# Expert products strip by strip, and the weights of expert 2 and of the last expert in whole loads

## What is computed

```python
# per expert e, for the tokens x routed to it
h = silu(x @ w_gate[e]) * (x @ w_up[e])     # w_gate, w_up: 1024 x 512
y = h @ w_down[e]                            # w_down: 512 x 1024
out = sum over the 2 experts of a token: gate weight * y
```

## Time and profile before

| | us |
|---|---|
| median of three timed runs | 4315.75 |
| lowest and highest of them | 4313.86, 4319.55 |
| the profiled execution, its own time | 4336.46 |
| its span in the trace | 4334.6 |
| PE busy (90% of the span) | 3896.4 |

### The profile page before, as it was taken

The page is one execution under the profiler, slowest core; times in us unless marked ns, Lnnn a source line. Parts: engine busy times, 40 slices in busy tenths (PEclk is TensorE's granted clock), DMA queues, the critical chain, the costliest instruction groups (busy, mean ns, idle before and its releaser), DMA issues. The chain is left out here.

```text
span 4334.6 us, 78138 instructions
## 1 busy us (share of the span) xinstructions
PE 3896.4 (90%) x33934; PEld 2475.1 (57%) x33934; DVE 2106.2 (49%) x3087; ACT 1006.4 (23%) x1749; POOL 620.7 (14%) x456
## 2 busy tenths in 40 slices
PE   7999998899999998999996999876999999699973
PEld 4555654445556545566544777543666665487742
DVE  3555356455555554555565222115666787422214
ACT  2333223133331221222210000003444541000002
POOL 2322011032211100000000211101221300111111
PEclk9999999999999999999997999987999999799986
DMA  4233202332231234544523999983000121699996
GB/s 131 95 108 99 62 20 88 86 112 93 98 98 30 88 108 133 88 78 79 105 85 123 377 417 380 419 356 101 16 1 16 40 70 75 236 417 391 403 424 269
DMA packets 260177, 694.97 MB, mean 160 GB/s; under 512 B 59467, under 2 KB 185043, under 8 KB 234103
## 3 DMA queue, kind: packets, MB, share of 16 engines
q1 hardware_dynamic: 245447, 645.79, 42.1%
q0 software_dynamic: 13056, 39.86, 2.5%
q10 hardware_dynamic: 1328, 4.24, 0.3%
HBM read 617.21 MB, written 64.08 MB: 157 GB/s over the span
## 5 line engine op out<-in xcount | busy, mean ns | idle before, releaser
L512 PE MATMUL ps<-sb_xT,sb_work 128*128 128x512 f32 x768 | 358.8, 605 | 8.6 <-ACT sb_x_tok L854 5.5
L512 PE MATMUL ps<-sb_mixT,sb_work 128*128 128x512 f32 x768 | 357.2, 602 | 8.6 <-ACT sb_x_tok L854 5.5
L2739 DVE TENSOR_TENSOR sb_work<-sb_work,ps 128x256 f32<-128x256 f32 (+2 forms) x66 | 33.6, 510 | 678.0 <-ACT sb_work L2726 678.0
L2726 ACT ACTIVATE sb_work<-ps 128x256 f32<-128x256 f32 (+2 forms) x66 | 30.0, 455 | 1032.6 <-PE ps L2694 1032.6
L1664 PE MATMUL ps<-sb_xT,sb_work 128*128 128x512 f32 x512 | 236.2, 600 | 0.0
L2694 PE MATMUL ps<-sb_work,sb_xT 128*32 128x256 f32 x3136 | 194.9, 398 | 37.0 <-DMA sb_work<-moe_w_up 23.3
L2694 PE MATMUL ps<-sb_work,sb_mixT 128*32 128x256 f32 x3136 | 196.1, 399 | 35.6 <-DMA sb_work<-moe_w_up 22.3
L512 PEld LDWEIGHTS ps<-sb_xT,sb_work 128*128 128x128 f32 x768 | 138.4, 192 | 148.3 <-issue 131.5
L512 PEld LDWEIGHTS ps<-sb_mixT,sb_work 128*128 128x128 f32 x768 | 138.0, 191 | 148.2 <-issue 131.4
L2709 PE MATMUL ps<-sb_work 128*32 128x256 f32 x3776 | 222.0, 379 | 0.0
L2151 DVE TENSOR_REDUCE sb_cols<-ps 128x1 f32<-128x1024 f32 x128 | 150.7, 1219 | 85.7 <-PE ps L1994 85.6
(11 more groups left out here) (497 smaller groups left out, 7019.1 us busy)
## 6 DMA issues: line engine op xcount, KB each, us to landing
sb_work<-moe_w_down SPq DMA_DIRECT2D x42, 2048.0 KB
sb_work<-moe_w_gate SPq DMA_DIRECT2D x30, 2048.0 KB
sb_work<-moe_w_up SPq DMA_DIRECT2D x30, 2048.0 KB
sb_xT<-moe_w_gate SPq DMA_DIRECT2D x15, 2048.0 KB
sb_xT<-moe_w_up SPq DMA_DIRECT2D x15, 2048.0 KB
sb_mixT<-moe_w_gate SPq DMA_DIRECT2D x15, 2048.0 KB
sb_mixT<-moe_w_up SPq DMA_DIRECT2D x15, 2048.0 KB
sb_work<-w_in SPq DMA_DIRECT2D x56, 512.0 KB, 4.3
```

The costliest lines, as they stand in the source:

```text
L512: last = pe.matmul(m.ps[:, bank, :], b.w[i][:, k, :], m.xT[:, k, half * HALF:(half + 1) * HALF], start=(k == 0), stop=(k == NK - 1))
L2726: act.activation(b.act[n % 2][:, 0:strips[n], :], strip_sums(2 + 2 * (n % 2))[:, 0:strips[n], 0:P], ACT.Silu).then_inc(silued, 1)
L2739: dve.tensor_tensor(act, act, strip_sums(2 + 2 * (n % 2))[:, 0:strips[n], P:2 * P], ALU.mult).then_inc(multiplied, 1)
```

## The change

`HALVED` and everything that belongs to it is gone. Gate and up of experts 2 and 31 are loaded like all others, in two transfers of 2 MB. Those of expert 2 wait for `up_ready` of product(0), where the first halves waited for `half_used`. `product` goes strip by strip: for each strip all 8 k tiles, for each k tile the four column tiles, with a start flag on each strip's first k. It waits once for its weights.

```diff
@@ expert_engines, product(n)
-            for half in range(2):
-                if loaded(n, 0, half):
-                    pe.wait_ge(*loaded(n, 0, half))
-                for k in range(half * NK // 2, (half + 1) * NK // 2):
-                    for g in range(strips[n]):
-                        for j in range(QUARTERS):
-                            last = pe.matmul(strip_sums(2 + 2 * (n % 2), tile[j])[:, g, :], b.x_turned[n % 2][:, g, k, :],
-                                             b.gate_up[weights[n] % 2][:, :, k, j * P:(j + 1) * P],
-                                             start=(k == 0 and g % 2 == 0),
-                                             stop=(k == NK - 1 and (g % 2 == 1 or g == strips[n] - 1)))
-                last.then_inc((half_used, up_ready)[half], 1)
+            if loaded(n, 0):
+                pe.wait_ge(*loaded(n, 0))
+            for g in range(strips[n]):
+                for k in range(NK):
+                    for j in range(QUARTERS):
+                        last = pe.matmul(strip_sums(2 + 2 * (n % 2), tile[j])[:, g, :], b.x_turned[n % 2][:, g, k, :],
+                                         b.gate_up[weights[n] % 2][:, :, k, j * P:(j + 1) * P], start=(k == 0), stop=(k == NK - 1))
+            last.then_inc(up_ready, 1)
@@ experts_stage, SP
             def load_gate_up(w):
-                sources = [by_rows(source(w, name)) for name in ("gate", "up")]
-                if w not in HALVED:
-                    for part in range(2):
-                        sp.dma_start(b.gate_up[w % 2][:, part, :, :], sources[part]).then_inc(gate_up_loaded[w % 2], 16)
-                    return
-                for half, landed in enumerate((gate_up_loaded[w % 2], second_loaded)):
-                    k = slice(half * NK // 2, (half + 1) * NK // 2)
-                    if w == HALVED[0]:
-                        sp.wait_ge((half_used, up_ready)[half], 1)
-                    for part in range(2):
-                        sp.dma_start(b.gate_up[w % 2][:, part, k, :], sources[part][:, k, :]).then_inc(landed, 16)
+                for part, name in enumerate(("gate", "up")):
+                    sp.dma_start(b.gate_up[w % 2][:, part, :, :], by_rows(source(w, name))).then_inc(gate_up_loaded[w % 2], 16)
...
             def gate_up_used(n):
                 if last_use(n) and WEIGHTS[n] + 2 < N_EXPERTS:
-                    if n:
-                        sp.wait_ge(up_ready, n + 1)
+                    sp.wait_ge(up_ready, n + 1)
                     load_gate_up(WEIGHTS[n] + 2)
```

More of the change, by code:

```diff
@@ L2257 @@
 LOADS, TURNS, WEIGHTS = weights_in_turn()
-HALVED = (2, N_EXPERTS - 1)
 def last_use(n):
@@ L2669, in expert_engines @@
     x_turned, up_ready, silued, multiplied, y_ready, y_copied = (s[f"signal_{n}"] for n in (0, 2, 3, 4, 5, 6))
-    h_turned, half_used = s["signal_11"], s["signal_13"]
+    h_turned = s["signal_11"]
     stored = s["stored"], s["prefetched"]
@@ L2703, in down @@
                 pe.wait_ge(y_copied, n - 1)
-            if loaded(n, 1, 0):
-                pe.wait_ge(*loaded(n, 1, 0))
+            if loaded(n, 1):
+                pe.wait_ge(*loaded(n, 1))
             for g in range(strips[n]):
@@ L2779, in experts_stage @@
     y_blocks = m.y_dram.rearrange("(p b) d -> p b d", p=P)
-    x_turned, up_ready, y_ready, y_copied, tokens_ready, second_loaded, half_used = (
-        s[f"signal_{n}"] for n in (0, 2, 5, 6, 7, 12, 13))
+    x_turned, up_ready, y_ready, y_copied, tokens_ready = (s[f"signal_{n}"] for n in (0, 2, 5, 6, 7))
     gathered = (m.pool_dma[l]["gathered_a"], m.pool_dma[l]["gathered_b"])
@@ L2848, in _, with loaded @@
                         m.slots[:, g, at:at + 1], 0)).then_inc(gathered[n % 2], 16)
-        def loaded(n, part, half):
+        def loaded(n, part):
             w = WEIGHTS[n]
[L2853 to L2859, removed]
+            if part == 0:
+                return (gate_up_loaded[w % 2], 32 * (w // 2)) if w >= 2 else None
+            return (down_loaded[w % 3], 16 * (w // 3 + (w % 3 == 2))) if w >= 2 else None
         expert_engines(nc, m, block, b, [strips_of(at) for at in TURNS], WEIGHTS, loaded,
@@ L2885, in _ @@
                         pool.sem_inc(tokens_ready, 1)
-                    expert_engines(nc, m, block, b, [4], [0], lambda n, part, half: ((gate_up_loaded, down_loaded)[part][0], (32, 16)[part]),
+                    expert_engines(nc, m, block, b, [4], [0], lambda n, part: ((gate_up_loaded, down_loaded)[part][0], (32, 16)[part]),
                                    lambda n: (tokens_ready, 1))
```

## The result

| | us |
|---|---|
| changed kernel, median of 20 runs (lowest, highest) | 4321.4 (4317.75, 4324.49) |
| kernel before, median of 20 runs beside it | 4315.76 (4312.59, 4319.55) |
| ratio, 95% interval | 1.0013 [1.0007, 1.0019] |
| the changed kernel's profiled execution, its span | 4320.81, 4318.9 |

The change costs 5.6 us. The whole interval lies above 1, so the kernel is slower, but by less than the 0.2% that the prediction took as no change; 11.4 us had been forecast. The profiled execution of the changed kernel is level with its median, while that of the kernel before was 20.7 us above its own. That turns out to matter.

What follows compares the result with a forecast made beforehand. Each expert stage was taken to start with PE and DMA balanced and end bound by loads, at expert 31's landing. 5.71 + 5.71 + 0 + 0 = 11.4 us on 4315.75 gave 4327.2 us, range 4319 to 4332.

Steps and rivals of the forecast that it cites:

- the clock holds: Rival, last product of each stage: PE keeps 2.4 GHz through the wait, 3.45 us per stage, 4322.7 us; chance 0.16.
- signs of being wrong: Whole kernel: last product at 7.11 us, product 2 waiting, three-strip products changing by over 0.1 us, or last landing moving.
- the late load: Rival, start of each stage: expert 2's load lands late and product 2 waits, 4331 to 4337 us; chance 0.10.
- slower by over 0.2%: Whole kernel: chance 0.70 of a time over 4324.4 us.
- The bound and the mechanism: End of each stage: expert 31's landing decides; the first half product must wait for it, costing 5.71 us per stage.
- The size of a product behind the wait: Last product of each stage: 9.37 us at a lowered clock, replacing 3.66 us after the landing.
- Expert 2: Start of each stage: loads leave 5.7 and 7.5 us later, hidden by slack of 1.4 and 1.5 us; cost 0.
- a hole to fill at 2402 us: DMA queues between experts 2 and 3: they run dry, 45 GB/s, and the later expert 2 load uses that bandwidth.
- Strip by strip: Loop order in every product: the array keeps its pace in either order; cost 0.
- "issue" stalls: Idle time in product, 7.9 us in the first stage; rival: strip order removes it, 4311.4 us; chance 0.07.
- The base of the sum: Whole kernel: the added 11.4 us, worked out on the 4336.46 us profile, applies equally to the timed median, 4315.75 us.
- The landing: End of each stage: expert 31's last load lands at the same distance from the stage's start; shift 0.

Runs made afterwards that it cites:

- c3: Kernel before with only expert 31 in whole loads (k outermost, expert 2 in halves), on a chip of the faster kind: 4325.22 us against 4315.89, ratio 1.0022.
- b1: Kernel before with only expert 31 in whole loads (k outermost, expert 2 in halves), on the slower chip: 4346.42 us against 4337.04, ratio 1.0024.
- a2: Changed kernel with product's loops put back to k outermost, experts 2 and 31 still in whole loads: 4320.82 us against 4315.62 before, ratio 1.0011.
- c1: Changed kernel again, no edit, beside three others on one chip: 4322.12 us against 4315.89 for the kernel before, ratio 1.0015.
- c2: Changed kernel plus 64 unused matmul instructions ahead of the wait for expert 31: 4318.71 us against 4315.89 for the kernel before, ratio 1.0006.
- a4: Changed kernel with expert 31 back in halves, its product k outermost with two waits: 4315.99 us against 4315.62 for the kernel before, ratio 1.0001.
- a1: Kernel before, unedited, run again for a second trace: 4315.16 us against 4315.62, ratio 1.0001; traced execution 4311.70 us.
- a3: Kernel before with strips outside k within each half product, experts 2 and 31 still in halves: 4314.55 us against 4315.62, ratio 1.0002.
- b3: Changed kernel plus 64 unused matmul instructions ahead of the wait for expert 31, on the slower chip: 4341.53 us against 4337.04 before, ratio 1.001.
- group b: Four edited kernels run together on one chip, where the kernel before took 4337.04 us; ratios from 0.9998 to 1.0027.

## Why the prediction was right and wrong

**The number** is right by half. 4321.4 us lies in the range of 4319 to 4332, but half of the forecast cost came, and the result lies within the 0.2% to which 0.26 was given. It is nearest to the rival "the clock holds" (4322.7 us), whose condition was not met: both last products of the traced execution took 8.80 us. The terms of the sum that the runs bear out make some 9.3 us; that only 5.6 were paid comes from something for which the prediction has no term. That the number still fell in the range owes as much to luck. Of the signs of being wrong that it had set, two came true: product 2 waited, and the three-strip products became shorter. Its chances do not add up either: the forecast (0.64) and the late load (0.10) both lie above 4324.4 us, so "slower by over 0.2%" had at least 0.74, not 0.70.

**The bound and the mechanism** were right. Both stages end at the landing of expert 31's gate and up, the half product that had run under the transfer moved behind it, and the clock fell in it. c3 and b1 isolate this step where expert 2 stays in halves: +9.3 and +9.4 us, against 11.4 forecast.

**The size of a product behind the wait** was taken too high. The step said 9.37 us, because all eight products with waits of 3.7 us or more had been slow. The ten last products in the profiles of the kernels with a whole last load and nothing ahead of it (the changed kernel, a2, b1, c1, c3) took 7.11 twice, 8.73, 8.80 four times, 8.96, 9.13 and 9.31: mean 8.56 us. With it the step is 8.56 - 3.66 = 4.9 us per stage and 9.8 in all, against 9.3 and 9.4 measured. The rule "3.7 us of wait or more, slow product" was a fit to eight cases and broke once in these ten: 7.11 us behind 3.88 (c3). Three of the ten waits were shorter, 2.01 to 3.40 us, and the six slow products behind the longer ones had a mean of 8.96 us, not 9.37. The rival "the clock holds" was right as an alternative within a stage and wrong as a case for both; c2 shows that its 1.7 us per stage are real.

**Expert 2.** The 0 held as a sum: a4 has this part and the order, and stays within its interval of the kernel before. The working behind it did not hold. In the five traces with the whole load on the faster kind of chip, product 2 waited 0.46 to 0.96 us in nine of ten stages (in a2's second it started 0.3 us late), since the slack of 1.4 us had been read from a trace with slower products. The delay was also not what I counted. On a chip of this kind SP is the later of the two in the first stage. In a1 the first half of product 0 (96 instructions) is done near 2381 us, and SP is still issuing small transfers:

```profile
2380.07 5.63 SPq L2823 DMA_DIRECT2D sb_cols<-scratch_mods  x2
2387.42 0.40 SPq L2806 DMA_DIRECT2D sb_work<-moe_w_gate  x1
```

so the first load leaves at 2387.42 in the kernel before and at 2387.93 in the changed one: 13.1 and 13.9 us after the first product's start, 0.8 us apart where 5.7 were forecast. In the second stage it leaves 7.5 and 13.1 us after that start (3727.31 and 3739.68), 5.6 us apart where 7.5 were forecast, and product 2 waited 0.89 us. Nor is there a hole to fill at 2402 us: where the earlier trace rows had 45 GB/s, the unchanged kernel in a1 moves

```profile
2402.00:2404.00 2.00, 2.00 (x44) 1.09 (x40) 1.27 (x2) 0.00 (x0) 1.39 (x3) 1.00 1.06 451
```

because product 1 ends earlier (its ACT step starts at 2397.54 in a1, at 2403.51 in the earlier trace rows) and expert 3's loads leave with it. In the second stage of a1 a dip is left, 154 GB/s from 3744 to 3746 us, where the earlier trace rows had 8.

**Strip by strip** was right at 0, by a2 and a3. The "issue" stalls were put down to neither order, and that was sound: the argument from the earlier trace rows, that a k-outer product without a stall exists, was the one that carried. The sign set for this step was bad. Three-strip products did become shorter than in the first trace, by more than the 0.1 us allowed, without the order having any part in it.

**The base of the sum.** The step "the profiled execution is 0.5% above the median, the added time is the same piece of PE work in both" passed over what this 0.5% was. By their level and by the stalls in the trace, the 20.7 us are the difference between the two kinds of chip told of below (on which chip that profile was taken is not recorded), and the rows about slack, issue times and holes came from the kind on which the timed runs did not run. For the main term it did no harm (b1 and c3 agree), for expert 2's terms it did.

**The landing** cannot be said to have moved. From first product to landing it was 516.07 and 517.44 us in a1, 515.46 and 515.53 in the changed kernel, 519.94 and 514.16 in the same kernel again.

**What stays open.** The last whole load alone costs 9.3 and 9.4 us; together with expert 2's whole load it costs 5.6, 6.2 (strips) and 5.2 (k outermost). Some 3 to 4 us are given back. The strip order is not needed for it, since a2 does not have it. Expert 2's whole load is what is left, but a4, which has it, gained nothing, and no profile shows where. The traces can't settle it. The two expert stages together last 1055.1 us (the changed kernel), 1058.7 (c1) and 1057.2 (a2), measured from the start of the first product to that of the last down, 1059.4 in c3, and 1047.4 in a1. But each is one execution: a1's stood 3.5 us below the median of its runs, c1's 4.1 above. Shifted by these distances (an estimate; 0.6 below for the changed kernel, 2.2 above for a2, 1.0 below for c3) the stages cost 4.8, 3.7 and 4.1 us more than in a1, and 9.5 in c3. So the traces do not speak against the medians. If the difference is real, the last landing would be the place to look for it: it comes 518.56 and 518.04 us after the first product in c3, and between 515.46 and 517.07 in the changed kernel and a2, but 519.94 and 514.16 in c1. A table of both experts, halved and whole, on one chip would tell whether it is more than scatter; it wasn't run. I don't call the cause of this part known.

## What to carry to other kernels

Cutting the last load of a stage bound by transfers, so that half of its work runs under the other half's transfer, is worth the hidden work plus what the idle engine loses in clock: here 9 us of 4316 with expert 2 in halves, and 5 to 6 with it whole. Cutting it finer gave nothing more that could be measured, and neither did the order of loops within a product that is fed at once. When the profiled execution stands well off the median of the timed runs, treat its slacks and stalls as those of another machine, and ask for a second trace before building on a slack of 1 us.

## What the runs showed of the hardware

**Two kinds of chip.** The same unchanged kernel takes 4315.6 us (33 runs, 4310.38 to 4319.15) on one chip, 4315.89 on a second and 4337.04 (31 runs, 4334.2 to 4341.5) on a third, without an overlap. The slower level was seen on one chip of three and in the first trace; that it belongs to the chip, and not to something else that stayed the same through a group of runs, is likely and not shown. The two expert stages make up 20.1 of the 24.7 us between the spans of the first trace and of a1: 534.09 and 533.39 us from the start of the first product to that of the last down in the first trace, 523.00 and 524.38 in a1. The granted clock is the same, and so is the DMA rate while the queues are full. In the window from 2500 to 2600 us, first a1 and then b1:

```profile
2500.00:2600.00 100.00, 92.48 (x1700) 65.89 (x1696) 22.59 (x23) 2.95 (x6) 14.61 (x16) 1.00 1.01 421
```

```profile
2500.00:2600.00 100.00, 95.83 (x1723) 84.46 (x1717) 24.50 (x25) 2.94 (x6) 16.41 (x17) 1.00 1.01 416
```

PE needs more time there for hardly more instructions, and its weight loads go from 65.89 to 84.46 us. A product of three strips is a row of 10.53 us on the one and mostly broken on the other (the earlier trace rows has one that is not), as here in b3, which has the strip order:

```profile
2411.37 8.64 PE L2696 MATMUL ps<-sb_work,sb_mixT 128*32 128x256 f32 x154 [0.77 <-issue]
```

All five traces at the 4337 us level have such pieces (the first one and the four of group b), in both orders; none of the nine at the 4316 us level has one. What in the chip differs, no row shows.

**The clock behind a wait is not a function of that wait.** The last product, 128 instructions, took from 7.11 to 9.56 us behind waits from 2.0 to 5.4 us. Filling the wait with 64 instructions gave 7.09 or 7.11 us in all four cases (b3 and c2, two stages each), in two of them behind a rest of the wait, of 1.17 and 2.33 us. The Trainium skill, page "TensorE: Matmul & The Clock Gate", section "HAM oscillation — how this bites in real kernels", has a DMA wait between bursts start each next burst cold. The traces agree that the clock falls around such waits, but show that the burst can start at the full clock and lose it on the way (in the first stage of the changed kernel 1.00 for a microsecond, then 0.50), and that sometimes it does not lose it at all (7.11 us behind a wait of 3.88 us in c3).
